# Grouped attention: the product with the values issued one step later, with two sets of turned probabilities

## Chip, cores and metric

The kernel runs on one core of a Trainium2 chip, all in 32-bit floats. The metric is the device time of one execution in microseconds (us), from launch to end; lower is better. Engines are called TensorE (PE, with its weight loads PEld), VectorE (DVE), ScalarE (ACT), GpSimd (POOL) and SyncE (SP, which issues DMA transfers).

## What is computed

The reference is two blocks of two layers each. The first has gated linear attention, the second a neighbourhood attention layer and a grouped-query attention layer, each with a mixture of experts behind it. The change touches only the grouped-query attention of the second block: 1024 tokens, 16 query heads of 64, in 4 groups that share one key and one value head each.

```python
def gqa_mixer(h, cos, sin, w_qkv, q_gain, k_gain, w_o):
    qkv = h @ w_qkv
    q, k, v = ...
    q = apply_axial_rope(rms_norm(q, q_gain), cos, sin)
    k = apply_axial_rope(rms_norm(k, k_gain), cos, sin)
    return block_gqa_attention(q, k, v) @ w_o

def one_block(qb):
    s = jnp.einsum('bqkgd,bskd->bkgqs', qb, k).astype(jnp.float32) * scale
    p = jax.nn.softmax(s, axis=-1).astype(v.dtype)
    return jnp.einsum('bkgqs,bskd->bqkgd', p, v)
```

## The kernel before

The kernel is a sequence of stages with a barrier between them. The grouped attention is one stage, `grouped_query_stage`. Each engine runs its own program in the order in which it is written, and they meet by semaphores. There is no scheduler: the order on each engine is the order of the code.

The stage has 64 steps, 16 for each of 4 groups. A step handles one tile of 128 queries for a pair of heads; `i` is the step and `n` its place (0 to 15) in the group. A step consists of:

- *Scores* (L1776, `scores`): TensorE multiplies queries with keys, 128 x 1024 for each of the two heads, into PSUM banks 0 to 3. It waits until both exponents of the step before (`exponent`, signal_8) have read those banks.
- *Maximum* (L1927, `find_top`): VectorE finds each row's maximum, for one head and then the other.
- *Exponent* (L1853, `exp`): ScalarE computes the exponentials and their sum. It waits for the maximum, and for the turn of two steps ago, which read the same buffer `prob[i % 2]`.
- *Normalisation* (L1932, L1935): VectorE takes the reciprocal of the sum and scales the probabilities.
- *Turn* (L1786, `turn`): TensorE transposes the probabilities of one head, four 128 x 128 blocks into bank 4 and four into bank 5. It waits for the normalisation (signal_10) and until the turn before it has been copied out of the bank (signal_13, signal_14).
- *Copy of the turned probabilities* (L1847 on ScalarE for bank 4, L1941 on VectorE for bank 5, `copy_out`) into `probT[head]`. There is one such buffer for each head, so both wait for the values' product of the step before (`weighed`, signal_15).
- *The values' product* (L1800, `weigh`): 16 matmuls of turned probabilities with values into bank 6, for both heads. It waits for all four copies of its step, and until the result of the step before has left bank 6 (`finished`, signal_16).
- *Copy-out* (L1946, `finish`): VectorE takes bank 6 to `mixT`.

On TensorE a step is: scores of step `i + 1`, turn of head 0, interleaved work, turn of head 1, interleaved work, the values' product. ScalarE's order is: copy of head 0, exponent of head 0 for step `i + 1`, evictions, copy of head 1, exponent of head 1 for step `i + 1`, evictions. VectorE's order is: maximum of head 0 (step `i + 1`), copy of head 0, maximum of head 1, copy of head 1, two normalisations of step `i + 1`, in places 6 and 11 a sum of squares (L1922), and the copy-out of step `i`.

The interleaved work is the projection of the next group (`project`, L1752) into bank 7: eight pieces of eight matmuls, and then six pieces of four transposes (L1762), which need the heads as GpSimd has rotated them (`roped`, signal_5; L1899 to L1914). Each piece waits until the one before has been evicted by ScalarE (`evicted`, signal_1; L1824, L1835). `GQA_UNITS` says how many units (two matmuls, or one transposed piece) stand behind the two turns of each place:

```python
GQA_UNITS = [(2, 1)] * 11 + [(2, 0), (0, 0), (0, 0), (2, 1), (0, 0)]
```

The last group has none. GpSimd's rotation of the second half of the tokens begins after the sum of squares and a square root in place 11, and the transposes of place 14 wait for its end. The first scores of the next group (issued in place 15) wait until all 14 pieces have been evicted.

Of the kernel before, what the change touches and what calls it, by code (L numbers as in the profile page):

```python
# [19 lines left out]
P = 128  # L20
SEQ = 1024
D = 1024
NT = SEQ // P
NK = D // P
HALF = 512
# [151 lines left out]
def more_memory(nc, m):  # L177
    def sb(name, shape, dt=F32):
        return nc.alloc_sbuf_tensor("sb_" + name, shape, dt)

    m.rows = sb("rows", [36, SEQ])
    m.a_log, m.dt_bias = sb("a_log", [36, 1]), sb("dt_bias", [36, 1])
    m.gate_w2 = sb("gate_w2", [64 + RANK, GLA_HEADS * GLA_DK])
    m.g_dram = nc.dram_tensor("scratch_g", [DEPTH, 8, SEQ], F32, kind="Internal").ap()
    m.x_dram = nc.dram_tensor("scratch_x", [SEQ, D], F32, kind="Internal").ap()
    m.one, m.eps6, m.eps5 = sb("one", [P, 1]), sb("eps6", [P, 1]), sb("eps5", [P, 1])
    m.conv, m.G_col, m.beta_col = sb("conv", [P, 52]), sb("G_col", [P, 4, NT]), sb("beta_col", [P, 4, NT])
    m.dn_g, m.gla_g, m.gate_b = m.conv[:, 48:49], m.conv[:, 49:50], m.conv[:, 50:52]
    m.cols, m.cols2 = sb("cols", [P, 64]), sb("cols2", [P, 64])
    m.stats, m.moments = sb("stats", [P, 2, 2, 6]), sb("moments", [P, NT, 2])  # L190
    m.mods = nc.dram_tensor("scratch_mods", [DEPTH, 6 * D], F32, kind="Internal").ap()
    m.gates, m.dest = sb("gates", [P, NT, TOP_K]), sb("dest", [P, TOP_K, NT], I32)
    m.overflow, m.slots = sb("overflow", [P, OVERFLOW + 1], I32), sb("slots", [P, N_BLOCKS], I32)
    m.index = sb("index", [P, 2], I32)
    m.h_dram = nc.dram_tensor("scratch_h", [SEQ, D], F32, kind="Internal").ap()
    m.y_dram = nc.dram_tensor("scratch_y", [P * N_BLOCKS, D], F32, kind="Internal").ap()
    m.bias_dram = nc.dram_tensor("scratch_bias", [64, 240, 64], F32, kind="Internal").ap()
    m.state, m.c_cols = sb("state", [P, 2, P]), sb("c_cols", [P, NK])
    m.v_tok, m.rope_gain = sb("v_tok", [P, 2, NT * HD]), sb("rope_gain", [P, 2 * HD + 512])

# [34 lines left out]
def advance(work, n):  # L235

    for _ in range(n):
        next(work, None)
# [1446 lines left out]
def grouped_query_stage(nc, m, a):  # L1685
# [8 lines left out]
    count, WIDE, n_norm = GQA_STEPS, (GROUP + 2) * HD, GROUP + 1  # L1694
    at = [0]

    def take(n):
        at[0] += n
        return m.work[:, at[0] - n:at[0]]
# [8 lines left out]
    q = [[take(SEQ) for _ in range(2)] for _ in range(2)]  # L1708
    k2 = [take(SEQ) for _ in range(2)]
    prob = [[take(SEQ) for _ in range(2)] for _ in range(2)]  # L1710
    probT = [take(SEQ) for _ in range(2)]
    v = [m.v_tok[:, n, :].rearrange("p (t d) -> p t d", d=HD) for n in range(2)]
    gain_q, gain_k = m.rope_gain[:, 0:HD], m.rope_gain[:, HD:2 * HD]
    rope = m.rope_gain[:, 2 * HD:2 * HD + 512].rearrange("p (t n) -> p t n", t=NT)
# [7 lines left out]
    with nc.Block() as block:  # L1722
# [18 lines left out]
        @block.tensor  # L1741
        def _(pe):
            def project(g):
                for n in range(GQA_PIECES):
                    piece = GQA_PIECES * g + n
                    if piece:
                        pe.wait_ge(evicted, piece)
                    if n == 0:
                        pe.wait_ge(loaded, 48 * (g + 1))
                    if n < NT:  # L1750
                        for k in range(NK):
                            last = pe.matmul(m.ps[:, 7, 0:WIDE], m.xT[:, k, n * P:(n + 1) * P], w[:, k, :],  # L1752
                                             start=(k == 0), stop=(k == NK - 1))
                            if k == NK - 1:
                                last.then_inc(projected, 1)
                            if k % 2 == 1:
                                yield
                    else:
                        half, j = divmod(n - NT, 3)
                        pe.wait_ge(roped, 2 * g + half + 1)  # L1760
                        for t in range(half_tiles):
                            last = pe.transpose(m.ps[:, 7, t * P:(t + 1) * P],  # L1762
                                                raw[:, half * half_tiles + t, j * P:(j + 1) * P], ident(m))
                        last.then_inc(projected, 1)
                        yield

            def scores(i):
                g, j, t = i // 16, i // NT % 2, i % NT
                if i:
                    pe.wait_ge(exponent, 2 * i)  # L1770
                if i % 16 == 0:
                    pe.wait_ge(evicted, GQA_PIECES * (g + 1))
                for half in range(2):
                    for head in range(2):
                        d = slice(64 * head, 64 * head + 64)
                        last = pe.matmul(m.ps[:, 2 * head + half, :], q[g % 2][j][d, t * P:(t + 1) * P],  # L1776
                                         k2[g % 2][d, half * HALF:(half + 1) * HALF], start=True, stop=True)
                last.then_inc(scored, 1)

            def turn(i, head):  # L1780
                pe.wait_ge(normalised, 2 * i + head + 1)
                for half, (copied, turned) in enumerate(((copied_4, turned_4), (copied_5, turned_5))):
                    if 2 * i + head:
                        pe.wait_ge(copied, 2 * i + head)
                    for b in range(4):
                        last = pe.transpose(m.ps[:, 4 + half, b * P:(b + 1) * P],  # L1786
                                            prob[i % 2][head][:, half * HALF + b * P:half * HALF + (b + 1) * P],
                                            ident(m))
                    last.then_inc(turned, 1)

            def weigh(i):
                g = i // 16
                pe.wait_ge(copied_4, 2 * i + 2)
                pe.wait_ge(copied_5, 2 * i + 2)
                pe.wait_ge(v_ready, 2 * (g + 1))
                if i:
                    pe.wait_ge(finished, i)
                for b in range(NT):
                    for head in range(2):
                        last = pe.matmul(m.ps[64 * head:64 * head + 64, 6, 0:P], v[g % 2][:, b, :],  # L1800
                                         probT[head][:, b * P:(b + 1) * P], start=(b == 0), stop=(b == NT - 1))
                last.then_inc(weighed, 1)

            for _ in project(0):
                pass
            scores(0)
            for i in range(count):
                g, n = divmod(i, 16)
                if n == 0:
                    work = project(g + 1) if g + 1 < KV_HEADS else iter(())  # L1810
                if i + 1 < count:
                    scores(i + 1)
                turn(i, 0)
                advance(work, GQA_UNITS[n][0])
                turn(i, 1)
                advance(work, GQA_UNITS[n][1])
                weigh(i)

        @block.scalar
        def _(act):  # L1820
# [21 lines left out]

            def copy_out(i, head):
                act.wait_ge(turned_4, 2 * i + head + 1)
                if i:
                    act.wait_ge(weighed, i)
                act.copy(probT[head][:, 0:HALF], m.ps[:, 4, :]).then_inc(copied_4, 1)  # L1847

            def exp(i, head):
                act.wait_ge(found, 2 * i + head + 1)  # L1850
# [15 lines left out]
            for i in range(count):  # L1866
                g, n = divmod(i, 16)
# [49 lines left out]
        def _(dve):  # L1917
# [18 lines left out]

            def copy_out(i, head):
                dve.wait_ge(turned_5, 2 * i + head + 1)
                if i:
                    dve.wait_ge(weighed, i)  # L1940
                dve.tensor_copy(probT[head][:, HALF:SEQ], m.ps[:, 5, :]).then_inc(copied_5, 1)  # L1941

            def finish(i):
                g, j, t = i // 16, i // NT % 2, i % NT
                dve.wait_ge(weighed, i + 1)
                dve.tensor_copy(m.mixT[:, 2 * g + j, t * P:(t + 1) * P], m.ps[:, 6, 0:P]).then_inc(finished, 1)  # L1946
# [9 lines left out]
            for i in range(count):  # L1956
                g, n = divmod(i, 16)
                if i + 1 < count:
                    find_top(i + 1, 0)
                copy_out(i, 0)  # L1960
                if i + 1 < count:
                    find_top(i + 1, 1)
                copy_out(i, 1)
                if i + 1 < count:
                    normalise(i + 1, 0)
                    normalise(i + 1, 1)
                if g + 1 < KV_HEADS and n in (6, 11):
                    sum_squares(g + 1, (6, 11).index(n))
                finish(i)
    end_stage(nc, m)  # L1970


# [711 lines left out]
```

## Time and profile before

| | us |
|---|---|
| median of three runs | 5220.67 (5218.51 to 5221.36) |
| the profiled execution, its own time | 5220.52 |
| its span, first to last instruction | 5218.7 |
| grouped attention stage, scores of step 0 to its last copy-out | about 3587 to 4172 of the span |
| mean granted TensorE clock, whole span | 0.953 |
| TensorE / VectorE / ScalarE / GpSimd busy over the span | 89% / 36% / 22% / 10% |

The page's first part gives busy time by engine, its second the span in slices, and its fifth the costliest groups of instructions. The stage is a ninth of the span, so the share of the whole tells little about it. The views that do are the waits of the stage, which add up an engine's idle time by what ended it, and the timeline, where each row is a run of equal instructions on one engine with its start, its busy time and, in brackets, the idle time before it and what released it. The span stands 1.8 us below the execution's time; this launch and end lie outside of the stage.

### The profile page before, as it was taken

To read this page: it belongs to the slowest core of one execution; us is meant where nothing else is said; L and a number is where in the kernel's file an instruction comes from. 1 tells how busy PE (TensorE), PEld (TensorE's weight loads), DVE (VectorE), ACT (ScalarE), POOL (GpSimd) and SP (SyncE) were. 2 spreads that over 40 slices of the span, in tenths; PEclk is the share of its full clock that TensorE was granted. 3 is DMA by queue.
4 is the path that set the end of the run, shared out by engine and by line. 5 is a ranking of instruction groups with operands and counts; after the bars stand their busy time and mean duration, and the time that the engine had idled before them with its cause. 6 is when DMAs were issued, how large, how long until landed. Compare 5 with 4: busy or idle time off the path is not lost. (4 is left out here: it accounts for less than half of the span.)

```text
span 5218.7 us, 51977 instructions
## 1 busy us (share of the span) xinstructions
PE 4647.9 (89%) x21250; PEld 2637.2 (51%) x21250; DVE 1858.3 (36%) x2765; ACT 1122.1 (22%) x1835; POOL 539.7 (10%) x382
## 2 busy tenths in 40 slices
PE   8999989899999989998969999957999896999993
PEld 4665654466665446665534444424666553444441
DVE  3332553433355334444511111133666662111114
ACT  2333121233322112222000000022444400000001
POOL 2221110132111000000000000012222000000001
PEclk9999999999999999998979999978999997999997
DMA  3111053210105311111269999830000035999993
GB/s 93 29 29 29 13 210 107 61 30 25 31 14 200 139 39 39 39 39 55 80 214 315 319 316 315 306 107 13 13 13 33 3 104 201 319 316 314 317 316 141
DMA packets 362683, 691.33 MB, mean 132 GB/s; under 512 B 53659, under 2 KB 139811, under 8 KB 362327
## 3 DMA queue, kind: packets, MB, share of 16 engines
q1 hardware_dynamic: 347143, 632.43, 35.8%
q0 software_dynamic: 14112, 51.39, 2.9%
q10 hardware_dynamic: 1200, 4.24, 0.2%
q8 instruction: 171, 2.80, 0.2%
q14 instruction: 57, 0.47, 0.0%
HBM read 624.20 MB, written 63.82 MB: 132 GB/s over the span
## 5 line engine op out<-in xcount | busy, mean ns | idle before, releaser
L2319 PE MATMUL ps<-sb_work,sb_xT 128*128 128x512 f32 x800 | 355.1, 597 | 40.6 <-DVE sb_xT L2379 40.6
L2319 PE MATMUL ps<-sb_work,sb_mixT 128*128 128x512 f32 x800 | 354.9, 597 | 40.5 <-DVE sb_mixT L2379 40.5
L2395 DVE TENSOR_TENSOR sb_work<-sb_work,ps 128x512 f32<-128x512 f32 x66 | 45.5, 689 | 962.0 <-PE ps L2319 962.0
L438 PE MATMUL ps<-sb_xT,sb_work 128*128 128x512 f32 x768 | 357.7, 602 | 9.0 <-ACT sb_x_tok L746 5.4
L438 PE MATMUL ps<-sb_mixT,sb_work 128*128 128x512 f32 x768 | 356.6, 601 | 7.4 <-ACT sb_x_tok L746 5.4
L2319 PEld LDWEIGHTS ps<-sb_work,sb_xT 128*128 128x128 f32 x800 | 148.9, 191 | 213.8 <-issue 169.0
L2319 PEld LDWEIGHTS ps<-sb_work,sb_mixT 128*128 128x128 f32 x800 | 148.7, 191 | 213.7 <-issue 169.0
L1468 PE MATMUL ps<-sb_xT,sb_work 128*128 128x512 f32 x512 | 239.3, 606 | 5.6 <-DMA sb_work<-na_w_qkv 5.6
L2339 PE MATMUL ps<-sb_mixT,sb_work 128*128 128x512 f32 x528 | 232.1, 592 | 0.9 <-ACT sb_work L2373 0.9
L2339 PE MATMUL ps<-sb_xT,sb_work 128*128 128x512 f32 x528 | 232.1, 592 | 0.9 <-ACT sb_work L2373 0.9
L2385 DVE TENSOR_TENSOR sb_work<-ps,sb_work 128x1024 f32<-128x1024 f32 x66 | 80.9, 1225 | 409.9 <-PE ps L2339 409.9
L438 PEld LDWEIGHTS ps<-sb_xT,sb_work 128*128 128x128 f32 x768 | 138.4, 192 | 146.0 <-issue 130.4
L438 PEld LDWEIGHTS ps<-sb_mixT,sb_work 128*128 128x128 f32 x768 | 138.0, 192 | 143.6 <-issue 129.6
L1752 PE MATMUL ps<-sb_work,sb_mixT 128*128 128x384 f32 x512 | 181.8, 493 | 21.3 <-DMA sb_work<-gqa_w_qkv 11.8
L1927 DVE TENSOR_REDUCE sb_cols<-ps 128x1 f32<-128x1024 f32 x128 | 156.1, 1220 | 124.4 <-PE ps L1776 124.4
L1092 DVE TENSOR_TENSOR sb_work<-sb_work,ps 128x1024 f32<-128x1024 f32 x40 | 48.9, 1221 | 353.7 <-PE ps L609 353.7
L2339 PEld LDWEIGHTS ps<-sb_xT,sb_work 128*128 128x128 f32 x528 | 100.2, 190 | 126.9 <-issue 125.8
L2339 PEld LDWEIGHTS ps<-sb_mixT,sb_work 128*128 128x128 f32 x528 | 100.2, 190 | 126.9 <-issue 125.8
L1800 PE MATMUL ps<-sb_work,sb_v_tok 128*64 128x128 f32 x2048 | 127.9, 278 | 33.6 <-ACT sb_work L1847 33.3
L1576 ACT ACTIVATE sb_work<-sb_work,sb_cols 128x512 f32<-128x512 f32 (+1 forms) x128 | 95.0, 743 | 287.3 <-DVE sb_cols L1622 287.3
L2373 ACT COPY sb_work<-ps 128x512 f32<-128x512 f32 x66 | 38.7, 587 | 539.2 <-PE ps L2328 539.2
L1786 PEld LDWEIGHTS ps<-sb_const,sb_work 128*128 128x128 f32 x1024 | 114.7, 143 | 76.4 <-issue 67.7
(425 smaller groups left out, 7455.2 us busy)
## 6 DMA issues: line engine op xcount, KB each, us to landing
sb_work<-moe_w_up SPq DMA_DIRECT2D x66, 2048.0 KB, 8.4
sb_work<-moe_w_gate SPq DMA_DIRECT2D x34, 2048.0 KB, 9.9
sb_xT<-moe_w_down SPq DMA_DIRECT2D x33, 2048.0 KB, 9.8
sb_mixT<-moe_w_down SPq DMA_DIRECT2D x33, 2048.0 KB, 9.8
sb_work<-ada_w SPq DMA_DIRECT2D x96, 512.0 KB, 6.3
scratch_y<-sb_work SPq DMA_DIRECT2D x82, 512.0 KB, 9.9
sb_xT<-moe_w_gate SPq DMA_DIRECT2D x16, 2048.0 KB, 9.0
sb_mixT<-moe_w_gate SPq DMA_DIRECT2D x16, 2048.0 KB, 9.0
```

The costliest lines, as they stand in the source:

```text
L438: last = pe.matmul(m.ps[:, bank, :], b.w[i][:, k, :], m.xT[:, k, half * HALF:(half + 1) * HALF], start=(k == 0), stop=(k == NK - 1))
L1092: dve.tensor_tensor(b.X, b.X, banks(m, 2), ALU.subtract).then_inc(x_ready, 1)
L1468: last = pe.matmul(m.ps[:, bank, :], w[j // 2][:, k, :], m.xT[:, k, j % 2 * HALF:(j % 2 + 1) * HALF], start=(k == 0), stop=(k == NK - 1))
L1576: act.activation(p, p, ACT.Exp, bias=top[:, column(i, head)], scale=-1.0, accum_out=total[:, column(i, head)]).then_inc(exponent, 1)
L1752: last = pe.matmul(m.ps[:, 7, 0:WIDE], m.xT[:, k, n * P:(n + 1) * P], w[:, k, :], start=(k == 0), stop=(k == NK - 1))
L1786: last = pe.transpose(m.ps[:, 4 + half, b * P:(b + 1) * P], prob[i % 2][head][:, half * HALF + b * P:half * HALF + (b + 1) * P], ident(m))
L1800: last = pe.matmul(m.ps[64 * head:64 * head + 64, 6, 0:P], v[g % 2][:, b, :], probT[head][:, b * P:(b + 1) * P], start=(b == 0), stop=(b = ...
L1927: dve.tensor_reduce(top[:, column(i, head)], banks(m, 2 * head), AX.X, ALU.max, negate=True).then_inc(found, 1)
L2319: last = pe.matmul(m.ps[:, 2 + 2 * (n % 2) + part, :], b.x_turned[n % 2][:, k * P:(k + 1) * P], w[:, k, :], start=(k == 0), stop=(k == NK ...
L2339: last = pe.matmul(m.ps[:, 6 + half, :], b.act_turned[n % 2][:, k * P:(k + 1) * P], b.down[n % 2][:, k, half * HALF:(half + 1) * HALF], st ...
L2385: dve.tensor_tensor(b.y[n % 2], banks(m, 6), b.gate_row, ALU.mult).then_inc(y_copied, 1)
L2395: dve.tensor_tensor(b.act[n % 2], b.act[n % 2], m.ps[:, 3 + 2 * (n % 2), :], ALU.mult).then_inc(multiplied, 1)
```

## The change

The values' product of step `i - 1` is issued in step `i`, between the interleaved work behind the turn of head 0 and the turn of head 1. The last product follows at the end. So that the turned probabilities of two steps can be held, `probT` becomes two sets, chosen by `i % 2`. Each set has four pieces of 512 columns. Five of the eight pieces lie in the old work buffer, and three in a new buffer `turned`. The copies into a set wait for the product of two steps ago. VectorE's copy-out moves by one step too: at the end of step `i` it takes the result of step `i - 1`.

```diff
+    m.turned = sb("turned", [P, 3 * HALF])
...
-    probT = [take(SEQ) for _ in range(2)]
+    pieces = [take(HALF) for _ in range(5)] + [m.turned[:, n * HALF:(n + 1) * HALF] for n in range(3)]
+    probT = [[pieces[4 * n + 2 * head:4 * n + 2 * head + 2] for head in range(2)] for n in range(2)]
...
-                                         probT[head][:, b * P:(b + 1) * P], start=(b == 0), stop=(b == NT - 1))
+                                         probT[i % 2][head][b // 4][:, b % 4 * P:(b % 4 + 1) * P], start=(b == 0), stop=(b == NT - 1))
...
                 turn(i, 0)
                 advance(work, GQA_UNITS[n][0])
+                if i:
+                    weigh(i - 1)
                 turn(i, 1)
                 advance(work, GQA_UNITS[n][1])
-                weigh(i)
+            weigh(count - 1)
...
-                if i:
-                    act.wait_ge(weighed, i)
-                act.copy(probT[head][:, 0:HALF], m.ps[:, 4, :]).then_inc(copied_4, 1)
+                if i >= 2:
+                    act.wait_ge(weighed, i - 1)
+                act.copy(probT[i % 2][head][0], m.ps[:, 4, :]).then_inc(copied_4, 1)
...
-                if i:
-                    dve.wait_ge(weighed, i)
-                dve.tensor_copy(probT[head][:, HALF:SEQ], m.ps[:, 5, :]).then_inc(copied_5, 1)
+                if i >= 2:
+                    dve.wait_ge(weighed, i - 1)
+                dve.tensor_copy(probT[i % 2][head][1], m.ps[:, 5, :]).then_inc(copied_5, 1)
...
-                finish(i)
+                if i:
+                    finish(i - 1)
+            finish(count - 1)
```

In the changed code the lines of this stage are numbered higher: the product is L1802 (before L1800), the scores L1778 (L1776), the turns L1788 (L1786), the transposed pieces L1764 (L1762), the exponent L1857 (L1853), the copies L1851 and L1945.

TensorE in a step of the last group, before; the signals are those named above, and signal_18 says that the values are in place:

```order
L1776 MATMUL ps<-sb_work 128x512 [waits signal_8]
L1776 MATMUL ps<-sb_work 128x512 x3
L1786 MATMUL ps<-sb_const,sb_work 128x128 [waits signal_13,signal_10]
L1786 MATMUL ps<-sb_const,sb_work 128x128 x3
L1786 MATMUL ps<-sb_const,sb_work 128x128 [waits signal_14]
L1786 MATMUL ps<-sb_const,sb_work 128x128 x3
L1786 MATMUL ps<-sb_const,sb_work 128x128 [waits signal_13,signal_10]
L1786 MATMUL ps<-sb_const,sb_work 128x128 x3
L1786 MATMUL ps<-sb_const,sb_work 128x128 [waits signal_14]
L1786 MATMUL ps<-sb_const,sb_work 128x128 x3
L1800 MATMUL ps<-sb_work,sb_v_tok 64x128 [waits signal_18,signal_16,signal_14,signal_13]
L1800 MATMUL ps<-sb_work,sb_v_tok 64x128 x15
```

TensorE in a step of the last group in the changed kernel:

```order
L1778 MATMUL ps<-sb_work 128x512 [waits signal_8]
L1778 MATMUL ps<-sb_work 128x512 x3
L1788 MATMUL ps<-sb_const,sb_work 128x128 [waits signal_13,signal_10]
L1788 MATMUL ps<-sb_const,sb_work 128x128 x3
L1788 MATMUL ps<-sb_const,sb_work 128x128 [waits signal_14]
L1788 MATMUL ps<-sb_const,sb_work 128x128 x3
L1802 MATMUL ps<-sb_work,sb_v_tok 64x128 [waits signal_18,signal_16,signal_14,signal_13]
L1802 MATMUL ps<-sb_work,sb_v_tok 64x128 x15
L1788 MATMUL ps<-sb_const,sb_work 128x128 [waits signal_13,signal_10]
L1788 MATMUL ps<-sb_const,sb_work 128x128 x3
L1788 MATMUL ps<-sb_const,sb_work 128x128 [waits signal_14]
L1788 MATMUL ps<-sb_const,sb_work 128x128 x3
```

The product has moved from behind the second turn to ahead of it, and the second turn is now the last work before the next scores.

TensorE in place 14 of the third group, from the second transposed piece to the first scores of the last group, before:

```order
L1762 MATMUL ps<-sb_const,sb_work 128x128 [waits signal_5,signal_1]
L1762 MATMUL ps<-sb_const,sb_work 128x128 x3
L1786 MATMUL ps<-sb_const,sb_work 128x128 [waits signal_13,signal_10]
L1786 MATMUL ps<-sb_const,sb_work 128x128 x3
L1786 MATMUL ps<-sb_const,sb_work 128x128 [waits signal_14]
L1786 MATMUL ps<-sb_const,sb_work 128x128 x3
L1762 MATMUL ps<-sb_const,sb_work 128x128 [waits signal_5,signal_1]
L1762 MATMUL ps<-sb_const,sb_work 128x128 x3
L1800 MATMUL ps<-sb_work,sb_v_tok 64x128 [waits signal_18,signal_16,signal_14,signal_13]
L1800 MATMUL ps<-sb_work,sb_v_tok 64x128 x15
L1776 MATMUL ps<-sb_work 128x512 [waits signal_1,signal_8]
L1776 MATMUL ps<-sb_work 128x512 x3
```

The same place on TensorE in the changed kernel, from the product on (the two transposed pieces stand ahead of it, as before):

```order
L1802 MATMUL ps<-sb_work,sb_v_tok 64x128 [waits signal_18,signal_16,signal_14,signal_13]
L1802 MATMUL ps<-sb_turned,sb_v_tok 64x128
...
L1802 MATMUL ps<-sb_turned,sb_v_tok 64x128 x9
L1788 MATMUL ps<-sb_const,sb_work 128x128 [waits signal_13,signal_10]
L1788 MATMUL ps<-sb_const,sb_work 128x128 x3
L1788 MATMUL ps<-sb_const,sb_work 128x128 [waits signal_14]
L1788 MATMUL ps<-sb_const,sb_work 128x128 x3
L1764 MATMUL ps<-sb_const,sb_work 128x128 [waits signal_5,signal_1]
L1764 MATMUL ps<-sb_const,sb_work 128x128 x3
L1778 MATMUL ps<-sb_work 128x512 [waits signal_1,signal_8]
L1778 MATMUL ps<-sb_work 128x512 x3
```

The product now stands between the second and the third transposed piece, with the turn of head 1, and the scores follow directly on the third piece.

## Rows read from the trace of the kernel before

**Rows 1.** Waits, 3588 to 4175 us: line, releaser, us in total, times, longest.

```profile
PE ps L1800 <- ACT sb_work L1847: 33.3, 31, 1.1
```

**Rows 2.** Timeline, last group: start, us busy, engine, line, [idle before <- releaser].

```profile
4088.51 1.97 PE L1800 MATMUL ps<-sb_work,sb_v_tok 128*64 128x128 f32 x32 [1.12 <-ACT sb_work L1847]
...
4090.41 1.99 PE L1776 MATMUL ps<-sb_work 64*128 64x512 f32 x8
...
4092.33 1.09 PE L1786 MATMUL ps<-sb_const,sb_work 128*128 128x128 f32 x8
...
4096.10 1.97 PE L1800 MATMUL ps<-sb_work,sb_v_tok 128*64 128x128 f32 x32 [1.12 <-ACT sb_work L1847]
```

**Rows 3.** Timeline, step 62's product and step 63's first turn.

```profile
4164.36 1.97 PE L1800 MATMUL ps<-sb_work,sb_v_tok 128*64 128x128 f32 x32 [1.12 <-ACT sb_work L1847]
...
4166.26 1.09 PE L1786 MATMUL ps<-sb_const,sb_work 128*128 128x128 f32 x8
...
4166.95 0.59 ACT L1847 COPY sb_work<-ps 128x512 f32<-128x512 f32 x1 [2.05 <-PE ps L1786]
```

**Rows 4.** Timeline, start of the stage: the second exponent and the scores behind it.

```profile
3590.87 1.12 ACT L1853 ACTIVATE sb_work<-ps,sb_cols 128x1024 f32<-128x1024 f32 x1
...
3592.13 3.40 PE L1776 MATMUL ps<-sb_work 64*128 64x512 f32 x8 [3.70 <-ACT sb_work L1853]
```

**Rows 5.** Timeline, a step of the second group with projection work.

```profile
3786.15 1.99 PE L1776 MATMUL ps<-sb_work 64*128 64x512 f32 x8
...
3788.07 1.09 PE L1786 MATMUL ps<-sb_const,sb_work 128*128 128x128 f32 x8
...
3788.99 2.75 PE L1752 MATMUL ps<-sb_work,sb_mixT 128*128 128x384 f32 x8
...
3791.58 1.04 PE L1786 MATMUL ps<-sb_const,sb_work 128*128 128x128 f32 x8
...
3792.21 0.59 ACT L1847 COPY sb_work<-ps 128x512 f32<-128x512 f32 x1 [1.56 <-PE ps L1786]
...
3792.45 1.46 PE L1752 MATMUL ps<-sb_work,sb_mixT 128*128 128x384 f32 x4
...
3792.70 1.12 ACT L1853 ACTIVATE sb_work<-ps,sb_cols 128x1024 f32<-128x1024 f32 x1
...
3793.84 1.97 PE L1800 MATMUL ps<-sb_work,sb_v_tok 128*64 128x128 f32 x32
```

**Rows 6.** Timeline, first group: place 11 and the start of place 12.

```profile
3701.92 1.99 PE L1776 MATMUL ps<-sb_work 64*128 64x512 f32 x8
...
3707.45 1.04 PE L1786 MATMUL ps<-sb_const,sb_work 128*128 128x128 f32 x8
...
3710.84 1.48 DVE L1922 TENSOR_REDUCE sb_cols<-sb_work 128x20 f32<-128x1280 f32 x1
3711.21 1.99 PE L1776 MATMUL ps<-sb_work 64*128 64x512 f32 x8
...
3713.00 2.33 POOL L1899 TENSOR_TENSOR sb_work<-sb_work,sb_cols 128x1280 f32<-128x1280 f32 x1 [12.61 <-ACT sb_cols L1841]
```

**Rows 7.** Timeline, place 14 of the first and third group, and the scores behind.

```profile
3731.34 0.89 PE L1762 MATMUL ps<-sb_const,sb_work 128*128 128x128 f32 x4 [1.95 <-POOL sb_work L1914]
...
3739.33 1.99 PE L1776 MATMUL ps<-sb_work 64*128 64x512 f32 x8
...
4038.06 0.63 PE L1762 MATMUL ps<-sb_const,sb_work 128*128 128x128 f32 x4 [1.96 <-POOL sb_work L1914]
...
4044.91 1.99 PE L1776 MATMUL ps<-sb_work 64*128 64x512 f32 x8
```

**Rows 8.** Windows, TensorE alone: stretch, its length, PE busy, PEclk, DMA, GB/s.

```profile
3733.00:3735.00 2.00, 2.00 (x10) 0.50 0.00 0
...
4040.00:4042.00 2.00, 2.00 (x12) 0.50 0.00 0
4042.00:4044.00 2.00, 1.67 (x23) 0.96 0.02 4
```

## The prediction

> **What bounds the kernel now.** I read the page for the stage's place in the span, then the waits of the stretch from 3588 to 4175 us, where the grouped attention runs, and then the timeline of single steps. The waits say what the change aims at: TensorE sits idle 33.3 us in all before the values' product, until the copies of the turned probabilities are done [rows 1]. A wait total does not tell which chain sets the length of a step, so the timeline has to. The 64 steps are of two kinds, and three of them are special.
>
> *Bare steps* (all of the last group, and places 12, 13 and 15 of the others, where no projection work is interleaved) take 7.59 us from one values' product to the next [rows 2]. TensorE works about 6.0 us of this. *Filled steps* (places 0 to 10 of the first three groups) carry projection matmuls as well and take 9.58 us: 3786.15 to the product at 3793.84, and 1.90 for the product [rows 3, 5]. TensorE has no idle time there; it is the bound. Three of each eleven are 0.9 longer, by a wait inside the projection that the change does not touch. *Place 14* of the first three groups takes 12.95, 12.95 and 11.82 us (start of its scores to the next): TensorE waits 1.95 for GpSimd's rotated heads, then runs on in part at a granted clock of 0.50, which is 1.2 GHz [rows 7, 8].
>
> **The new chain of a step.** The change takes the wait at the values' product away: what it reads was copied a step ago. But in the kernel before, the product stands behind the second turn, and while it runs, ScalarE copies the turned half and computes the second exponent, for which the next scores wait. With the product moved ahead of the second turn, that cover is gone: from the second turn on only the projection unit is left to TensorE, and in bare steps nothing. The chain from the second turn's start to the next scores is: turn to ScalarE's copy 0.69 (4166.26 to 4166.95, a turn that follows a product, as now all second turns do) [rows 3]; copy to exponent 0.49 (3792.21 to 3792.70) [rows 5]; exponent to scores 1.26 (3590.87 to 3592.13, the one place of before where the scores wait for it) [rows 4]. Together **2.44 us**.
>
> **Part 1, bare steps.** Up to the second turn TensorE now needs scores 1.92 (4090.41 to 4092.33) [rows 2], first turn 0.92 (3788.07 to 3788.99) [rows 5], product 1.90 (4164.36 to 4166.26) [rows 3]: 4.74. With the chain 2.44 a step lasts 7.18, against 7.59: 0.41 less, though the wait removed is 1.12 in the step shown. The rest is a new wait, about 1.5 us before the scores. There are 14 such steps of the last group (its last two apart) and place 15 of three groups: 17 x 0.41 = **-7.0**. By the nearest rows the first turn could cost 1.09 (its whole busy time) and the start of the copy 0.63 (3791.58 to 3792.21) [rows 5], so 0.2 to 0.5 a step: -3.4 to -8.5. VectorE's second maximum, on which the exponent also waits, ends 5.0 us after the scores start, and the exponent begins at 5.9.
>
> **Part 2, filled steps.** Up to the second turn: 1.92 + 0.92, the eight projection records, the product 1.90. The eight take 2.59 ahead of a turn, and the four ahead of the product 1.39 (3792.45 to 3793.84) against 1.30 for half of 2.59, so 2.69 [rows 5]. That is 7.43, and 9.87 with the chain, against 9.59: **0.28 more**. What TensorE has left behind the second turn, the turn and four projection records, is 2.26 (3791.58 to 3793.84), less than 2.44 [rows 5]. 30 steps of places 0 to 9, less the very first: 29 x 0.28 = **+8.1**. Bounds: nothing, if TensorE's 2.26 covers the chain and the change of neighbours costs nothing, and 0.35; so 0 to +10. Place 10 lasts 9.83 before and so about the same after. Place 11 has transposes with waits between, and its second turn starts 5.53 after its scores (3701.92 to 3707.45) [rows 6]; before it lasts 9.29 (to 3711.21), after 5.53 + 1.90 + 2.44 = 9.87. 3 x 0.58 = **+1.7**.
>
> **Part 3, places 12 to 14.** GpSimd's rotation starts 1.79 after the scores of place 12 (3711.21 to 3713.00), since VectorE's sum of squares starts 0.37 ahead of these scores (3710.84) [rows 6]. In the changed kernel the exponent of the second head ends as the scores start, and the normalisation between it and the sum (a reciprocal of 0.15 and a scaling of 0.75 with their gaps) puts the sum 0.84 behind the scores: 1.21 later. From GpSimd's start to TensorE's first transposes of place 14 are 18.34 us (to 3731.34) [rows 6, 7] that do not change. So the 0.41 of places 12 and 13 gives nothing, and this point comes **1.21** later; TensorE's wait there grows from 1.95 to about 4.1. Behind it, before: the product 1.86 after the second turn (in place 11, 9.29 - 5.53 - 1.90), and 1.90 for itself, 3.76. After: 1.90 + 2.44, and 0.55 more, because the scores of the next group also wait for ScalarE's eviction of the last piece, which stands in its queue behind the exponent: 4.89. **+1.13**. The clock: from these transposes to the next group's scores are 7.99 us in the first two groups (3731.34 to 3739.33) and 6.85 in the third (4038.06 to 4044.91) [rows 7]; by the parts at full clock (1.30 and 0.5 for the two transposed pieces, 3.76) it would be 5.57, so the low clock costs 1.3 to 2.4 now. With a longer idle time ahead and the product inside the low stretch I take 0.9 more (bounds 0.8 less and 3 more: no row shows a wait of 4 us here). Sum 3.25 a group, **+9.8** for three, bounds +4.6 to +16.
>
> The trace shows the clock back (0.50, then 0.96) before the product of place 14 in the third group has begun, after nothing but transposes [rows 8]. The Trainium skill ("TensorE: Matmul & The Clock Gate", Part 4, on PE-mode transpose) says that transposes do not count as busy for the clock in the way matmuls do. By that rule the product, which now comes ahead of the second turn, would lift the clock earlier, the 0.9 would fall away, and the time would be 5230 rather than 5233. The row speaks against the rule here, so the 0.9 stands.
>
> **Part 4, the ends and the rest.** The first step loses its product (-1.9, and +0.1 for the chain), the last has one ahead of its second turn and VectorE's copy-out ahead of the final one (+1.6): **-0.2**. The extra set of buffers costs no instruction: every copy and product is the same in number and shape. No DMA is moved: SyncE's loads wait for projected pieces, and are far ahead. VectorE's copy-out of a step back stands after its two normalisations and ends about 1.2 after the scores, and the next product starts 2.8 after them, so it costs nothing, unless that queue is over 1.6 late.
>
> **Sum.** -7.0 + 8.1 + 1.7 + 9.8 - 0.2 = **+12.4 us** on the profiled execution's 5220.52, which is 0.15 from the median of the runs, 5220.67. Forecast **5233 us**.
>
> **Rivals.**
> *A, the chain is covered in the filled steps.* If the chain from the second turn takes 2.26 or less, part 2's filled steps cost nothing, and 4.3 is left: 5225, no change. The point that decides is 2.26 against 2.44; for it speaks that the 1.26 was read where ScalarE had just been waiting, against it that each link has a row. 0.2.
> *B, the boundaries do not grow.* If GpSimd starts as early as before, the 1.21 and the 0.9 for the clock fall away: 12.4 - 3 x 2.11 = +6.1, 5227. 0.12.
> *C, the change does what it says.* The 33.3 us of [rows 1] go and nothing comes: 5187, faster. It asks for the exponents to be ready when the second turn ends, 1.5 us earlier than the rows allow. 0.04. A smaller gain, with A and B both true and the bare steps at their better bound (-8.5 + 1.7 + 3.4 - 0.2), gives -3.6: still within 0.2%.
> *D, the low clock spreads.* If 4 us of waiting hold TensorE at 1.2 GHz through the product, the turn and the next scores, each boundary costs another 3 us: 5242. 0.14.
> *Forecast as summed*, with its middle bounds: 0.45. What is left, 0.05, is for what I have not seen.
>
> **How the numbers follow.** About 0.2%, 10.4 us, is what a measurement of this kernel can tell from no change, so slower begins at 5231.1. The forecast's own range, 5226 to 5239, lies to two thirds above it, 0.30; D adds 0.14, and half of the 0.05 and a part of A and B (with the other terms at their upper bounds) 0.08: slower 0.52. Faster: C and a little of the rest, 0.06. Same 0.42. The range takes in A, B and D: 5219 to 5244.
>
> **What would show it.** In the changed kernel the scores (L1778) should show an idle time for ScalarE's exponent (L1857) in nearly every step, about 1.4 us in bare and 0.2 in filled ones, some 30 us in all, and the product (L1802) none for copies. Bare steps should start 7.18 apart, filled ones 9.87, place 14 over 15 us, with over 3.5 us of waiting for GpSimd. The forecast is wrong if filled steps stay at 9.59 (A), if place 14 stays below 14 (B), or if the scores do not wait (C).

## The result

| | before | changed |
|---|---|---|
| median, 15 runs each | 5220.86 us (5217.95 to 5223.77) | 5231.79 us (5227.85 to 5237.12) |
| the profiled execution, its own time | 5220.52 | 5236.28 |
| its span | 5218.7 | 5234.5 |
| clock over the span | 0.953 | 0.952 |

The ratio is 1.0024, with a 95% interval of 1.0016 to 1.0031: slower by 10.9 us. The forecast was 5233 us.

The profiled executions stand 15.8 us apart, more than the medians. The stage explains 12.2 of that: from its first scores to the next stage's first matmul are 588.3 us before (3584.75 to 4173.06; the table ahead of the prediction has about 3587 for the first scores, which is 2 too late) and 600.5 after (3587.41 to 4187.90). 2.7 us were already there when the stage began, where the code is the same, and about 0.9 came behind it. Such shifts go with the execution: in the profiles of the experiments below the stage's first scores start anywhere from 3582.2 to 3585.1, also where the kernel has the new buffer. So steps are compared inside the stage.

The waits of the stage in the changed kernel (3588 to 4190 us; waiting engine and line, releaser, total, times, longest):

```profile
PE ps L1778 <- ACT sb_work L1857: 41.4, 30, 3.7
PE ps L1764 <- POOL sb_work L1918: 11.3, 3, 3.8
...
PE ps L1778 <- ACT sb_work L1839: 5.1, 4, 1.5
```

The product's wait for the copies, 33.3 us in [rows 1], is gone. So is a second wait for ScalarE's copy, ahead of the second turn, that the kernel before had and the prediction did not name:

```profile
PE ps L1786 <- ACT sb_work L1847: 8.3, 25, 0.3
```

In their place the scores wait 41.4 us for ScalarE's exponent; only 3.7 of that, at the start of the stage, was there before. The wait for GpSimd rose from 5.9 us (three of 1.95) to 11.3, and the scores wait for the eviction of the last piece.

A bare step of the last group in the changed kernel (timeline; start, busy, engine, line, [idle before]):

```profile
4106.18 1.99 PE L1778 MATMUL ps<-sb_work 64*128 64x512 f32 x8 [1.34 <-ACT sb_work L1857]
...
4108.10 1.09 PE L1788 MATMUL ps<-sb_const,sb_work 128*128 128x128 f32 x8
...
4109.12 1.97 PE L1802 MATMUL ps<-sb_work,sb_v_tok 128*64 128x128 f32 x32
...
4111.02 1.09 PE L1788 MATMUL ps<-sb_const,sb_work 128*128 128x128 f32 x8
4111.71 0.59 ACT L1851 COPY sb_turned<-ps 128x512 f32<-128x512 f32 x1 [1.03 <-PE ps L1788]
...
4112.19 1.12 ACT L1857 ACTIVATE sb_work<-ps,sb_cols 128x1024 f32<-128x1024 f32 x1
...
4113.45 1.13 PE L1778 MATMUL ps<-sb_work 64*128 64x512 f32 x4 [1.35 <-ACT sb_work L1857]
```

Read it down from 4111.02. Once the second turn starts, TensorE has nothing else to do: the copy begins 0.69 later, the exponent 0.48 after that, and the scores 1.26 after that, 2.43 in all, against 2.44 forecast from [rows 3 to 5]. The step lasts 7.27 instead of the 7.59 of [rows 2].

A filled step of the second group in the changed kernel:

```profile
3792.74 1.99 PE L1778 MATMUL ps<-sb_work 64*128 64x512 f32 x8
...
3794.66 1.09 PE L1788 MATMUL ps<-sb_const,sb_work 128*128 128x128 f32 x8
...
3795.59 2.75 PE L1754 MATMUL ps<-sb_work,sb_mixT 128*128 128x384 f32 x8
...
3798.27 0.32 PE L1802 MATMUL ps<-sb_work,sb_v_tok 128*64 128x128 f32 x1
...
3800.17 1.09 PE L1788 MATMUL ps<-sb_const,sb_work 128*128 128x128 f32 x8
3800.86 0.59 ACT L1851 COPY sb_work<-ps 128x512 f32<-128x512 f32 x1 [3.62 <-PE ps L1788]
...
3801.09 1.46 PE L1754 MATMUL ps<-sb_work,sb_mixT 128*128 128x384 f32 x4
...
3801.34 1.12 ACT L1857 ACTIVATE sb_work<-ps,sb_cols 128x1024 f32<-128x1024 f32 x1
...
3802.60 0.70 PE L1778 MATMUL ps<-sb_work 64*128 64x512 f32 x2
```

It lasts 9.86 (3792.74 to 3802.60), where that of [rows 5] lasts 9.59. The scores start 1.26 after the exponent here too. The idle time of TensorE is so short that the view does not print it beside the matmul.

The boundary of the groups, place 14. GpSimd's rotation starts 3.18 behind the scores of place 12 (1.79 in [rows 6]), and the transposes wait longer for its end. The rotation is shown from the first group, the transposes from the third:

```profile
3715.47 1.99 PE L1778 MATMUL ps<-sb_work 64*128 64x512 f32 x8 [1.35 <-ACT sb_work L1857]
...
3718.65 2.33 POOL L1903 TENSOR_TENSOR sb_work<-sb_work,sb_cols 128x1280 f32<-128x1280 f32 x1 [15.11 <-ACT sb_cols L1845]
```

```profile
4054.11 0.63 PE L1764 MATMUL ps<-sb_const,sb_work 128*128 128x128 f32 x4 [3.77 <-POOL sb_work L1918]
...
4062.51 0.70 PE L1778 MATMUL ps<-sb_work 64*128 64x512 f32 x2 [1.48 <-ACT sb_work L1839]
```

From these transposes to the next group's scores are 8.40 us, against 6.85 in [rows 7]. Place 14 lasts 15.11, 16.39 and 15.18 us in the three groups (12.95, 12.95 and 11.82 before).

All steps of the stage together, from the starts of the scores:

| term | before | changed | number | measured | forecast |
|---|---|---|---|---|---|
| bare steps | 7.585 | 7.28 | 17 | -5.2 | -7.0 |
| filled steps, places 0 to 9 | 9.585 | 9.86 | 29 | +8.0 | +8.1 |
| place 10 | 9.84 | 9.86 | 3 | +0.1 | 0 |
| place 11 | 9.29 | 9.95 | 3 | +2.0 | +1.7 |
| places 12 to 14 together | 28.1, 28.1, 27.0 | 29.7, 30.9, 29.7 | 3 | +7.1 | +9.8 |
| first and last step | | | 2 | +0.2 | -0.2 |
| sum | | | | +12.2 | +12.4 |

(Three of each ten filled steps are 0.89 longer in both kernels, and are counted by their difference.)

### The profile page after: what moved, and what is told of

It is laid out like the page before. It is cut to its first block and busy times, and to the rows that moved or that the text cites. A ratio compares the mean times of both kernels' runs of the same rounds, so it can differ in the third digit from the quotient of the medians.

```text
span 5234.5 us, 51973 instructions
## 1 busy us (share of the span) xinstructions
PE 4653.6 (89%) x21250; PEld 2634.0 (50%) x21250; DVE 1854.8 (35%) x2765; ACT 1120.5 (21%) x1835; POOL 537.3 (10%) x382
## 5 line engine op out<-in xcount | busy, mean ns | idle before, releaser
L2325 PE MATMUL ps<-sb_work,sb_mixT 128*128 128x512 f32 x800 | 356.2, 598 | 41.4 <-DVE sb_mixT L2385 41.4
L1778 PE MATMUL ps<-sb_work 64*128 64x512 f32 x512 | 130.6, 629 | 48.1 <-ACT sb_work L1857 41.4
L1857 ACT ACTIVATE sb_work<-ps,sb_cols 128x1024 f32<-128x1024 f32 x128 | 143.1, 1118 | 13.7 <-DVE sb_cols L1931 8.4
```

Of the source, the lines that this page charges most:

```text
L1857: act.activation(prob[i % 2][head], banks(m, 2 * head), ACT.Exp, bias=top[:, column(i, head)], accum_out=total[:, column(i, head)]).then_i ...
L2325: last = pe.matmul(m.ps[:, 2 + 2 * (n % 2) + part, :], b.x_turned[n % 2][:, k * P:(k + 1) * P], w[:, k, :], start=(k == 0), stop=(k == NK ...
```

## The experiments

Theory: what counts for the product is not how old its input is, but which work of TensorE stands behind the second turn. Rivals: the wait for copies was what mattered; the second set of buffers costs something; the product costs TensorE more among projection matmuls; the boundaries between groups are bound by a chain of their own, and not by GpSimd's end. All runs below are compared with runs of the kernel before on the same chip, and a difference to the changed kernel is put together from its 10.9 us and such a comparison.

### The product a step late, but behind the second turn

```diff
                 turn(i, 0)
                 advance(work, GQA_UNITS[n][0])
-                if i:
-                    weigh(i - 1)
                 turn(i, 1)
                 advance(work, GQA_UNITS[n][1])
+                if i:
+                    weigh(i - 1)
             weigh(count - 1)
```

> Two sets and the product of the step before, as in the change, but issued behind the second turn, where the product stood before. Theory (the product's place uncovers the second exponent): the product runs while ScalarE copies and exponentiates, and its own inputs are a step old. The second exponent then starts when the second maximum ends, 5.0 us behind the scores, and the next scores 1.26 later: bare steps 6.3 us instead of 7.59, filled steps 9.59 as before. About 14.5 bare steps of the last group and place 15 of three groups gain 1.3 each, places 12 and 13 nothing (GpSimd), some 24 us in all: 5197. Rival (any delay of the product by a step costs, because VectorE's copy-out or the mixed buffers are slower): filled steps 9.86 here too, total not below 5221.

Measured: 5196.19 us, ratio 0.9953 (0.9939 to 0.9967). Filled steps 9.59, bare steps of the last group 6.40 where 6.3 was expected. The kernel gains 23.8 us on the one before (5220.01 in the same comparison). Places 12 to 14 give none of it: the wait for GpSimd grew to 4.1 us in each group, and place 14 lasts 14.4 to 14.9. Its timeline in the last group:

```profile
4104.89 1.23 PE L1788 MATMUL ps<-sb_const,sb_work 128*128 128x128 f32 x8 [0.33 <-ACT sb_work L1851]
...
4105.95 0.58 ACT L1851 COPY sb_turned<-ps 128x512 f32<-128x512 f32 x1
...
4106.05 1.97 PE L1802 MATMUL ps<-sb_work,sb_v_tok 128*64 128x128 f32 x32
...
4106.57 1.12 ACT L1857 ACTIVATE sb_work<-ps,sb_cols 128x1024 f32<-128x1024 f32 x1
...
4107.94 1.99 PE L1778 MATMUL ps<-sb_work 64*128 64x512 f32 x8
```

The product starts as soon as the second turn is through, with no wait, and runs while ScalarE copies and exponentiates. When it is done, so is the exponent, and the scores follow with no idle time in front. The same buffers and the same product of the step before as in the change, moved by one turn, make about 35 us of difference (23.8 less, where the change is 10.9 more). That refutes the rival by which lateness or the mixed buffers cost time.

### The two sets alone

```diff
                 turn(i, 0)
                 advance(work, GQA_UNITS[n][0])
-                if i:
-                    weigh(i - 1)
                 turn(i, 1)
                 advance(work, GQA_UNITS[n][1])
-            weigh(count - 1)
+                weigh(i)
...
-                if i:
-                    finish(i - 1)
-            finish(count - 1)
+                finish(i)
```

> Only the two sets of turned probabilities, with the product of step i at its old place at the end of step i. Theory: the single set never made a copy wait, so nothing changes: 5221 within 1.5, bare steps 7.59, filled 9.59. Rival (the new buffer or its addresses cost time, and are part of the change's loss): slower by 3 us or more.

Measured: 5220.09 us, ratio 0.9999 (0.9990 to 1.0008), filled steps 9.59, bare ones 7.58 to 7.59, place 14 12.95, 12.98 and 11.82. The second set by itself neither costs nor gains: it is room for a move, not a gain.

### The exponent ahead of the copy

```diff
                 copy_out(i, 1)
-                if i + 1 < count:
-                    exp(i + 1, 1)
...
+                if i + 1 < count:
+                    exp(i + 1, 1)
                 copy_out(i, 1)
```

> The changed kernel, with one line moved on ScalarE: the exponent of the second head stands ahead of the copy of the second turn, and so no longer behind the turn. Theory (the chain from the second turn to copy, exponent and next scores bounds the changed kernel): the chain is cut, the exponent starts when the second maximum ends. Bare steps 6.3 to 6.5 us, filled steps TensorE-bound at 9.6 to 9.7, no idle time of the scores in filled steps. Against the changed kernel 29 x 0.2 + 17 x 0.85 = 20 us less: about 5212. Rival (the filled steps are longer because the product between projection matmuls costs TensorE itself more): filled steps stay at 9.86, and only the bare ones gain, 5218.

Measured: 5210.55 us, ratio 0.9982 (0.9973 to 0.9991), about 20 us below the changed kernel. Bare steps of the last group alternate between 6.28 and 6.45. Places 12 to 14 took some of the gain back: TensorE waits 4.3 for GpSimd, and place 14 lasts 15.4 to 16.3. Filled steps are 9.73 to 9.74, so they come down, but only by 0.12, and not to 9.59. The timeline of one:

```profile
3791.43 1.11 ACT L1857 ACTIVATE sb_work<-ps,sb_cols 128x1024 f32<-128x1024 f32 x1 [0.53 <-DVE sb_cols L1931]
...
3793.82 1.09 PE L1788 MATMUL ps<-sb_const,sb_work 128*128 128x128 f32 x8
...
3794.75 1.46 PE L1754 MATMUL ps<-sb_work,sb_mixT 128*128 128x384 f32 x4
...
3796.14 1.99 PE L1778 MATMUL ps<-sb_work 64*128 64x512 f32 x8
```

The exponent is done 3.5 us before the scores, and TensorE runs without a pause. So 9.74 is what the new order of its work costs TensorE itself, and both theories hold in part: of the 0.28 of a filled step about 0.12 is the exponent's wait and 0.15 the new neighbours. The rows show where the 0.15 comes from. Eight projection records take 2.68 ahead of the product (3795.59 to 3798.27 above) and 2.59 ahead of a turn [rows 5], 0.09 more; a turn that follows the product holds TensorE for 0.93 (3793.82 to 3794.75), one that follows projection matmuls 0.87 (3791.58 to 3792.45) [rows 5], 0.06 more.

### The change in the last group alone

```diff
-                if i:
+                if i > 48:
                     weigh(i - 1)
                 turn(i, 1)
                 advance(work, GQA_UNITS[n][1])
+                if i < 48:
+                    weigh(i)
             weigh(count - 1)
...
-                if i:
+                if i < 48:
+                    finish(i)
+                elif i > 48:
                     finish(i - 1)
             finish(count - 1)
```

> The change in the last group alone (steps 48 to 63); the first three groups keep the product at the end of its own step. Theory (terms of the sum): 14 bare steps at 7.28 for 7.59 are -4.3, the step without a product -1.3, the last step +1.9: 3.7 less than before, 5217, and the three other groups' filled steps and boundaries, which cost +16, are as before. Rival (the wait for copies is what the change saves): 15 x 1.12 = 17 less, 5204.

Measured: 5217.80 us, ratio 0.9994 (0.9985 to 1.0003). The time alone cannot be told from no change, and rules out the 17 us of the rival. The steps say more: 9.59 and 12.96 in the first groups as before, 6.28 in the step without a product, then one of 8.91, and 7.27 to 7.28 in all others. The 8.91 was not expected. The windows of TensorE around it (stretch, length, busy, clock):

```profile
4052.00:4054.00 2.00, 1.67 (x13) 1.00 0.00 0
4054.00:4056.00 2.00, 0.58 (x4) 1.00 0.00 0
4056.00:4058.00 2.00, 1.71 (x6) 0.69 0.00 0
4058.00:4060.00 2.00, 2.00 (x6) 0.50 0.00 0
4060.00:4062.00 2.00, 2.00 (x28) 0.95 0.00 0
```

The step without a product left TensorE idle for 1.71 us after one pause of 0.33, and behind it the clock was at 1.2 GHz for some 3.4 us, which took back what that step had won.

### The root one place earlier, in three kernels

The boundaries were tested by letting GpSimd start earlier, first in the changed kernel:

```diff
-                    if n in (6, 11):
-                        take_root(g + 1, (6, 11).index(n))
+                    if n in (5, 10):
+                        take_root(g + 1, (5, 10).index(n))
...
-                if g + 1 < KV_HEADS and n in (6, 11):
-                    sum_squares(g + 1, (6, 11).index(n))
+                if g + 1 < KV_HEADS and n in (5, 10):
+                    sum_squares(g + 1, (5, 10).index(n))
```

> The changed kernel, with the sum of squares and the root of each half issued one place earlier (places 5 and 10 instead of 6 and 11), so that GpSimd's rotation of the second half starts about 9.9 us earlier. Theory (the three boundaries are set by GpSimd's end, and cost a wait of 3.75 us and a stretch at low clock): the wait and the low clock go, place 14 comes down from 15.1, 16.4 and 15.2 to about 9.5 us, 18 us less than the changed kernel: 5213. Rival (place 14 is bound by its own chain of transposes, evictions and exponents, and the wait for GpSimd only overlaps it): place 14 stays over 13 us and the gain is under 8 us.

Measured: 5218.89 us, ratio to before 0.9998 (0.9989 to 1.0007), about 12 us below the changed kernel where 18 was expected. Place 14 is 10.52 in all three groups, and the wait for GpSimd is gone. Place 11 rose from 9.95 to 10.52: the sum and the root now stand at the end of place 10, the first exponent of place 11 starts 3.86 behind its scores instead of 3.29, and the second transposed piece waits 2.15 for the eviction behind that exponent instead of 1.58. Place 14 came out 1 us longer than expected, mostly because the eviction of the first transposed piece now has to wait for the first exponent, which stands ahead of it in ScalarE's queue:

```profile
3729.54 0.60 PE L1764 MATMUL ps<-sb_const,sb_work 128*128 128x128 f32 x4
3729.98 1.11 ACT L1857 ACTIVATE sb_work<-ps,sb_cols 128x1024 f32<-128x1024 f32 x1
3731.00 0.19 ACT L1857 ACTIVATION_READ_ACCUMULATOR sb_work<-ps,sb_cols 128x1 f32 x1
3731.09 0.58 ACT L1839 COPY sb_work<-ps 128x512 f32<-128x512 f32 x1
3731.72 0.66 PE L1764 MATMUL ps<-sb_const,sb_work 128*128 128x128 f32 x4 [1.58 <-ACT sb_work L1839]
```

The next transposes start 2.18 behind the first instead of 1.30. Where TensorE had waited for GpSimd, that exponent had run under the wait.

The same edit in the kernel before:

> The kernel before, with only the root one place earlier. Theory: the wait of 1.95 us for GpSimd and the low clock behind it go, place 14 falls from 12.95, 12.95 and 11.82 to about 8.4 us: 12 us less than before, 5208.5. Rival (the low clock in place 14 comes from the transposes, and not from the wait ahead of them): the clock is low there still, and the gain is under 7 us.

Measured: 5210.56 us, ratio 0.9982 (0.9973 to 0.9991), 9.8 us gained where 12 were expected, with place 14 at 9.29 and not 8.4, as here too the second transposes start 2.18 behind the first. All windows of TensorE in place 14 show a clock of 1.00, through the same transposes and with a wait of 1.58 us for the eviction:

```profile
3728.00:3730.00 2.00, 0.42 (x4) 1.00 0.00 0
3730.00:3732.00 2.00, 1.63 (x15) 1.00 0.00 0
```

So the low clock of place 14 comes with the wait for GpSimd, and not with the transposes.

And with the product behind the second turn:

> The product of the step before behind the second turn, and the root one place earlier as well. Theory (the two effects are independent and add): from 5196.2 another 19 us, as place 14 falls from 14.4 to 14.9 to about 8.2 us: 5177. Rival (with the bare steps shortened, GpSimd is again late for place 14): place 14 over 11 us, 5186 or more.

Measured: **5180.45 us**, ratio 0.9924 (0.9911 to 0.9938), the fastest version: 40 us below the kernel before and 51 below the changed one. Place 14 is 8.84, 8.84 and 8.85, and places 12 and 13 are 6.40, which had been 6.49 and 7.13 with the product's place alone. The rival, GpSimd late again, does not occur: of the waits of this stage none is for GpSimd any more. Place 11 of the third group lasted 10.40 instead of 8.78, at a low clock (its second transposed piece; then windows of TensorE):

```profile
3993.26 0.66 PE L1764 MATMUL ps<-sb_const,sb_work 128*128 128x128 f32 x4 [1.98 <-ACT sb_work L1839]
```

```profile
3994.00:3996.00 2.00, 2.00 (x16) 0.52 1.03 412
3996.00:3998.00 2.00, 2.00 (x26) 0.63 0.21 82
```

The same wait of 1.98 stands in place 11 of the other two groups, where the clock stayed at 1.00. Why it fell in one of the three is not shown.

## Why the prediction was right

**What bounds a step.** The prediction's first step, that the wait total of [rows 1] does not tell what a step costs and that the product covered the second exponent, is shown by the first and third experiment: move the product behind the turn, or the exponent ahead of the copy, and bare steps go from 7.28 to 6.40 and to 6.28 to 6.45. The chain of 2.44, put together from three links at three places in the trace, measured 2.43.

**Part 1**, -7.0, measured -5.2. The mechanism held; one link was mis-sized by 0.10. I took 0.92 for the first turn, from a row where projection matmuls follow it [rows 5]. With the product behind it, it is 1.02 (4108.10 to 4109.12). The bound of 1.09 covered this.

**Part 2**, +8.1, measured +8.0. The size was right, but a part of the reasoning was not: the prediction had TensorE with 2.26 of work behind the second turn and put the lower bound of a filled step's loss at nothing. TensorE's own order already costs 0.15, as the third experiment shows. The prediction's own rows gave 0.10 of that (7.43 + 2.26 against 9.59), which the bound and rival A left out. Rival A (5225) could not have come out as it was stated: with the chain covered the filled steps still lose 29 x 0.15 = 4.4 us. Place 11 measured +2.0 for +1.7.

**Part 3**, +9.8, measured +7.1. GpSimd's start behind the scores moved by 1.39 for the 1.21 forecast, and the transposes by 1.18 (20.13 to 21.31 in the first group) for 1.21. TensorE waits 3.74 to 3.77 for the 4.1 forecast (by its own terms, 1.95 + 1.21 + 2 x 0.41, it would be 3.98, and places 12 and 13 gave 0.31 each and not 0.41). Behind the transposes 1.13 for the product and the eviction and 0.9 for the clock were forecast; measured are 0.37, 1.62 and 1.55 (8.36, 9.61 and 8.40 for 7.99, 7.99 and 6.85), 1.18 on average. The two terms can be told apart, because with the root earlier both kernels ran this stretch at full clock: 6.44 (3727.46 to 3733.90) in the kernel before and 7.67 (3729.54 to 3737.21) in the changed one, 1.23 more. So the 1.13 was short by 0.10, and the clock's 0.9 is the mis-sized term: what is left for it is -0.86, +0.39 and +0.32, nothing on average. The windows of TensorE over these stretches, three of the kernel before and three of the changed one (stretch, length, busy, clock):

```profile
3731.34:3739.33 7.99, 7.31 (x52) 0.57 0.00 0
3884.70:3892.69 7.99, 7.31 (x53) 0.57 0.01 2
4038.06:4044.91 6.85, 5.84 (x52) 0.75 0.01 1
```

```profile
3736.78:3745.14 8.36, 6.21 (x53) 0.80 0.01 2
3894.82:3904.43 9.61, 7.46 (x53) 0.64 0.00 0
4054.11:4062.51 8.40, 6.25 (x52) 0.80 0.01 3
```

By these means (twice what the clock lacks to 1.00, times the length) 6.9, 6.9 and 3.4 us were at 0.50 before, and 3.3, 6.9 and 3.4 in the changed kernel. The wait had doubled, but the time at the low clock did not grow. The rule of the Trainium skill ("TensorE: Matmul & The Clock Gate", Part 4), that transposes do not count as busy in the way matmuls do, would have dropped this term, and it did come out at nothing. The runs do not show that it is for that reason: in the kernel before the clock came back after transposes alone [rows 8], and in the second group of the changed one it stayed at 0.50 through the whole product (3897.43 to 3901.04).

**Part 4** and the rest: the ends +0.2 for -0.2, and the second set costs nothing (second experiment). Rival B, boundaries that do not grow, and rival C, the gain of 33.3 us, are refuted by the traces; for D, a low clock that spreads, no boundary showed the 3 us more.

**The net** of +12.2 in the profiled pair against +10.9 between the medians lies within what single executions differ by. That the sum came this close is partly luck: part 1 gained 1.8 us less than forecast and part 3 cost 2.7 less, and these two errors cancel in the main.

## What to carry to other kernels

In a software pipeline over several engines, ask of each block of TensorE work what runs beneath it on the other engines before it is moved: a wait in front of a block can be cheaper than the cover that the block gives. The place for work whose inputs are long ready is behind the last instruction that starts the other engines' chain; moved there, the same product gained 23.8 us where it had lost 10.9. And a side chain (here GpSimd's rotation) that ends just in time eats the gains of the steps before it, until its start is moved as well.

## What the runs showed of the hardware

- The length of a single wait did not decide whether TensorE's clock fell. A clock of 0.50 came behind a wait of 1.71 us ahead of the scores, in a step without its product (last group alone), and behind each wait of 1.95 for GpSimd in the kernel before. But a wait of 2.15 in place 11 of the changed kernel with the root earlier left it at 1.00 in all three groups, as did one of 1.58 in place 14, and one of 1.35 in each of 14 successive steps of 7.28 us in the changed kernel. Equal waits went both ways: 1.98 in place 11 of the fastest version (two at 1.00, one followed by 0.50), and 1.64 ahead of the stage's last turn of head 0 (1.00 in the changed kernel, 0.50 behind it with the exponent ahead of the copy). What decides is not shown. The clock over the last group of the changed kernel:

```profile
4063.00:4172.00 109.00, 88.81 (x842) 1.00 0.00 1
```

- Handing TensorE over from one kind of work to another has a price that depends on the pair: eight transposes hold it for 0.87 to 0.93 us ahead of projection matmuls and for 1.02 ahead of the product, whose matmuls write 64 x 128 each.
